# The last pair of expert quads gets an order of its own, and its last weights come in column halves

## The reference, cut to what matters

```
a = jnp.einsum('btd,edf->btef', h, w_gate)        # 1024 -> 256, 32 experts
b = jnp.einsum('btd,edf->btef', h, w_up)
act = jax.nn.silu(a) * b * combine[..., None]
moe = jnp.einsum('btef,efd->btd', act, w_down)    # 256 -> 1024
x = x + moe
y = rmsnorm(x, final_norm_w)
```

## Time and profile before

| what | value |
|---|---|
| median of 3 runs | 655.6 us (653.7 to 657.87) |
| the profiled execution, its own time | 657.37 us |
| its span (first to last instruction) | 655.7 us |
| mean granted TensorE clock | 0.955 of full |
| busy share of the span | PE 88%, DVE 39%, ACT 22%, POOL 11% |
| moved by DMA | 156.44 MB, mean 239 GB/s |

### The profile page before, as it was taken

How to read it: one execution, slowest core, us unless ns; L and a number is a source line. 1 busy time by engine, 2 the same in 40 slices (tenths; PEclk the granted TensorE clock), 3 DMA queues, 4 the chain that set the end, 5 groups by cost and what they waited for, 6 DMA issues and landing times.

```text
span 655.7 us, 11160 instructions
## 1 busy us (share of the span) xinstructions
PE 575.9 (88%) x4490; PEld 401.3 (61%) x4490; DVE 255.6 (39%) x696; ACT 146.1 (22%) x409; POOL 71.6 (11%) x164
## 2 busy tenths in 40 slices
PE   5999999888999999999869999999949677696974
PEld 4777777665777775567757688875434435253531
DVE  4464445651433616234452224544404040404134
ACT  3255333224552001123320013300000000000003
POOL 5000000022411090000100042210000000000000
PEclk8999999999999999999979999999969797988998
DMA  9943333447824062239235892689999999999961
GB/s 265 324 141 95 118 119 120 136 144 190 236 81 153 10 210 73 66 106 278 67 96 178 322 405 108 254 337 421 410 420 422 419 421 420 421 422 419 385 257 73
DMA packets 79435, 156.44 MB, mean 239 GB/s; under 512 B 11042, under 2 KB 64407, under 8 KB 66910
## 3 DMA queue, kind: packets, MB, share of 16 engines
q1 hardware_dynamic: 56880, 142.68, 57.6%
q10 hardware_dynamic: 22505, 13.05, 7.3%
HBM read 147.95 MB, written 7.95 MB: 238 GB/s over the span
## 4 chain that ended last, share of the span: by engine, by line
PE 68%; DMA 22%; DVE 4%; issue 1%; SPq 1%; ACT 1%; ACTq 1%; DVEq 0%
PE ps L1091 30%; DMA arena<-in_w_up_dram 18%; PE ps L1612 7%; PE ps L1471 5%; PE ps L1489 4%; PE ps L1427 2%; PE ps L1053 2%; DMA arena<-in_w_down_dram 2%; PE ps L1668 2%; PE ps L1622 2%; DMA arena<-in_w_in_dram 2%; PE ps L1684 1%; SPq L431 1%; PE ps L1237 1%; PE ps L1201 1%
## 5 line engine op out<-in xcount | busy, mean ns | idle before, releaser
L1091 PE MATMUL ps<-arena 128*128 128x288 f32 x832 | 221.4, 416 | 2.7 <-DMA arena<-in_w_in_dram 2.7
L1091 PEld LDWEIGHTS ps<-arena 128*128 128x128 f32 x832 | 154.0, 192 | 49.3 <-issue 4.9
L1612 PE MATMUL ps<-arena 128*32 128x256 f32 x1024 | 68.6, 430 | 35.8 <-DMA arena<-in_w_up_dram 34.8
L1612 PEld LDWEIGHTS ps<-arena 128*32 128x32 f32 x1024 | 39.6, 124 | 63.6 <-issue 49.7
L1053 PE MATMUL ps<-arena 128*128 128x128 f32 (+6 forms) x172 | 33.2, 300 | 18.5 <-DVE arena L2260 4.7
L1772 DVE SCALAR_TENSOR_TENSOR arena<-arena 128x312 f32<-128x312 f32 x72 | 39.2, 544 | 2.5
L1053 PEld LDWEIGHTS ps<-arena 128*128 128x128 f32 (+6 forms) x172 | 22.0, 156 | 29.2 <-issue 13.1
L1622 PE MATMUL ps<-arena 128*128 128x128 f32 x336 | 38.6, 275 | 0.0
L1622 PEld LDWEIGHTS ps<-arena 128*128 128x128 f32 x336 | 38.1, 192 | 0.0
L1668 PE MATMUL ps<-arena 128*32 128x512 f32 x256 | 30.8, 623 | 3.9 <-DMA arena<-in_w_down_dram 3.9
L1471 PE MATMUL ps<-arena 128*128 128x288 f32 x128 | 31.3, 407 | 0.9 <-DVE arena L2105 0.9
(11 more groups left out here) (368 smaller groups left out, 642.3 us busy)
## 6 DMA issues: line engine op xcount, KB each, us to landing
arena<-in_w_gate_dram SPq DMA_DIRECT2D x32, 1024.0 KB, 18.2
arena<-in_w_up_dram SPq DMA_DIRECT2D x32, 1024.0 KB, 18.5
arena<-in_w_down_dram SPq DMA_DIRECT2D x32, 1024.0 KB, 18.5
arena<-in_w_in_dram SPq DMA_DIRECT2D x26, 1024.0 KB, 5.4
arena<-in_w_branch_delta_dram SPq DMA_DIRECT2D x4, 1024.0 KB, 5.4
out_dram<-arena ACTq DMA_DIRECT2D x8, 512.0 KB, 4.0
arena<-in_w_out_dram SPq DMA_DIRECT2D x4, 1024.0 KB, 5.3
arena<-in_state_delta_dram ACTq DMA_DIRECT2D x7, 512.0 KB, 7.1
```

The lines of the kernel that those rows point to most:

```text
L1091: last = mm(ps[n % 2][:, 0:T], w[:, k, P * (n % 2):P * (n % 2) + P], hT[:, k, :], start=(k == 0), stop=(k == KD - 1))
L1612: last = mm(to[CAP * e:CAP * e + CAP, 0:FE], xgT[u][:, k, CAP * e:CAP * e + CAP], w[e][:, k, :], start=(k == 0), stop=(k == KD - 1))
```

## The change: what it does

For the last pair alone, three things. TensorE's order becomes: gates 6, gather of quad 7, ups 6, flips 6, gates 7, down 6, way back 6, ups 7, flips 7, first half of down 7, pieces 0 and 1, second half of down 7, pieces 2 to 4. ScalarE and VectorE follow in orders that fit. The down weights of quad 7 go into the slots of the even gates, which are free after gates 6, so SyncE waits on `m_gate` rather than on `m_dn1`. And each of those four tables comes in two loads of 512 KiB, first the columns 0 to 511 of all four experts, then the columns 512 to 1023, with a semaphore for each half.

```diff
+LAST_DOWNS = EVEN_GATES
...
-            ups_downs(end * 2 - 1, ((end - 1) % (QUADS // 2)) * (2 * QE) + QE)
+            last = ((end - 1) % (QUADS // 2)) * (2 * QE) + QE
+            ups(end * 2 - 1, last)
+            sp.wait_ge(S["m_gate"], end * 2 - 1)
+            for half in range(2):
+                cols = slice(512 * half, 512 * half + 512)
+                for e, s in enumerate(LAST_DOWNS):
+                    src = w_down[0, bass.ds(last + e, 1)].rearrange("e a b -> (e a) b")
+                    sp.dma_start(slots[s].rearrange("p (a n) -> p a n", a=2)[:, :, cols],
+                                 src.rearrange("(p a) n -> p a n", a=2)[:, :, cols]).then_inc(S[f"last_in{half}"], 16)
...
+            def last_pair(i):
+
+                q = 2 * i
+                gate_silu(q, 0)
+                rows_in(q + 1, 1)
+                flipped(q, 0)
+                gate_silu(q + 1, 1)
+                down_evac(q)
+                flipped(q + 1, 1)
+                down_evac(q + 1)
...
+            def last_pair(i):
+
+                q = 2 * i
+                gate_products(i, 0)
+                gather_next(q)
+                up_products(i, 0)
+                act_flips(q, 0)
+                gate_products(i, 1)
+                pe.wait_ge(S["m_aTev"], q + 1)
+                pe.wait_ge(S["m_dnA"], q)
+                pe.wait_ge(S["m_dnV"], q)
+                loaded(DOWNS, i, 0)
+                for half in range(2):
+                    down_half(0, DOWNS, half)
+                way_back(q, 0, range(NY))
+                up_products(i, 1)
+                act_flips(q + 1, 1)
+                pe.wait_ge(S["m_aTev"], q + 2)
+                pe.wait_ge(S["last_in0"], 16 * QE)
+                down_half(1, LAST_DOWNS, 0)
+                way_back(q + 1, 1, range(2))
+                pe.wait_ge(S["last_in1"], 16 * QE)
+                down_half(1, LAST_DOWNS, 1)
+                way_back(q + 1, 1, range(2, NY))
...
+            def last_pair(i):
+
+                q = 2 * i
+                rows_in(q + 1, 1)
+                gated_rows(q, 0)
+                down_evac(q)
+                add_pieces(q, 0, range(NY))
+                next_place(q * TURN + FIRST_TURNS)
+                way_back(q * TURN + (FIRST_TURNS + 1))
+                gated_rows(q + 1, 1)
+                add_pieces(q + 1, 1, range(2))
+                down_evac(q + 1)
+                add_pieces(q + 1, 1, range(2, NY))
```

More of the change, by code:

```diff
@@ L437, in gates, with ups @@
                     part_load(q, w_gate, first + e, s)
-            def ups_downs(q, first):
+            def ups(q, first):
                 sp.wait_ge(S["m_up"], q)
@@ L442, in ups_downs @@
                     part_load(q, w_up, first + e, s)
+            def ups_downs(q, first):
+                ups(q, first)
                 sp.wait_ge(S["m_dn1"], q)
@@ L1008, in quad_acts, with flipped, down_evac @@
                 nc.scalar.activation(sg[u], ps[2][:, 0:FE], ACT.Silu).then_inc(S["m_sg"], 1)
+            def flipped(q, u):
                 act.wait_ge(S["m_aT"], q + 1)
                 nc.scalar.activation(actT[u].rearrange("p c t -> p (c t)"), ps[4][:, 0:FE], ACT.Copy).then_inc(S["m_aTev"], 1)
-                if not final:
-                    rows_in(q + 1, 1 - u)
+            def down_evac(q):
                 act.wait_ge(S["m_dn0"], q + 1)
@@ L1028, in _ @@
                     quad_acts(i, u)
-            for u in range(2):
-                quad_acts(end - 1, u, final=(u == 1))
+            last_pair(end - 1)
             nc.scalar.activation(t4[:, 0, 0:1], t4[:, 0, 0:1], ACT.Sqrt)
@@ L1634, in spot_rows, with gate_products @@
                     last.then_inc(S["rows_pe"], 1)
-            def quad_products(i, u, final=False):
+            def gate_products(i, u):
                 q = 2 * i + u
@@ L1644, in quad_products, with act_flips @@
                 products(i, u, UPS, ps[3]).then_inc(S["m_up"], 1)
[L1645 to L1648, removed]
+            def act_flips(q, u):
                 pe.wait_ge(S["m_act"], q + 1)
@@ L1654, in quad_products, with down_half, way_back @@
                 last.then_inc(S["m_aT"], 1)
[L1655 to L1674, removed]
+            def down_half(u, table, half):
+                for c in range(2):
+                    for e in range(QE):
+                        w = slots[table[e]].rearrange("p (c n) -> p c n", c=2)
+                        last = mm(ps[5 + half][CAP * e:CAP * e + CAP, :], actT[u][:, c, CAP * e:CAP * e + CAP],
+                                  w[:, c, 512 * half:512 * half + 512], start=(c == 0), stop=(c == 1))
+                last.then_inc(S[f"m_dn{half}"], 1)
+            def way_back(q, u, pieces):
+                for j in pieces:
+                    t, half = PIECES[j]
                     bank = ps[4 if (NY * u + j) % 2 else 7]
+                    if j == 0:
+                        pe.wait_ge(S["m_back"], q + 1)
+                        pe.wait_ge(S["m_dnA"], q + 1)
                     wait_from(S["m_yadd"], q * NY + (j - 1))
@@ L1695, in _ @@
                     quad_products(i, u)
-            for u in range(2):
-                quad_products(end - 1, u, final=(u == 1))
+            last_pair(end - 1)
             pe.wait_ge(S["m_yadd"], end * (2 * NY))
@@ L2252, in next_place, with gated_rows @@
                 dve.wait_ge(S["turns"], turns + 1)
-            def quad_acts(i, u, final=False):
-                q = 2 * i + u
+            def gated_rows(q, u):
                 dve.wait_ge(S["m_sg"], q + 1)
@@ L2261, in quad_acts, with down_evac, add_pieces @@
                                 ps[3][:, 0:FE].rearrange("p (q c) -> p c q", c=2), ALU.mult).then_inc(S["m_act"], 1)
+            def down_evac(q):
+                dve.wait_ge(S["m_dn1"], q + 1)
+                wait_from(S["m_y"], q * NY)
+                V.tensor_copy(dn[:, 512:1024], ps[6][:, :]).then_inc(S["m_dnV"], 1)
+            def add_pieces(q, u, pieces):
+                for j in pieces:
+                    t, half = PIECES[j]
+                    bank = ps[4 if (NY * u + j) % 2 else 7]
+                    dve.wait_ge(S["m_y"], q * NY + (j + 1))
+                    v = x2s if t == 2 else x2[:, t, 512 * half:512 * half + 512]
+                    V.tensor_tensor(v, v, bank[:, 0:v.shape[1]], ALU.add).then_inc(S["m_yadd"], 1)
+            def quad_acts(i, u):
+                q = 2 * i + u
+                gated_rows(q, u)
                 if isinstance(q, int) and q == 0:
@@ L2267, in quad_acts @@
                     way_back(1 + NT)
[L2268 to L2279, removed]
+                rows_in(q + 1, 1 - u)
+                down_evac(q)
+                add_pieces(q, u, range(NY))
                 next_place(q * TURN + FIRST_TURNS)
```

30 lines of the change are left out of this document (28 added, 2 removed).

## The result

| what | before | after |
|---|---|---|
| median of 20 runs each, side by side | 658.91 us | 654.81 us |
| lowest | 653.7 us | 650.89 us |
| the profiled execution, own time | 657.37 us | 653.19 us |
| its span | 655.65 us | 651.47 us |
| mean granted TensorE clock | 0.955 | 0.961 |

The ratio is 0.9941, with a 95% interval of 0.992 to 0.9962: 0.6% faster, or 3.9 us of 658.91. The sign was forecast, and the case "within 1%" was the likelier one; the forecast of 6.3 us was too large, and 654.81 lies outside the range of 647.7 to 652.0. One run of each kernel lies far above the rest (706.17 and 1886.05 us); these two count as slow and are left out of the ratio. One part of that gap is no part of the change: the kernel before has a median of 658.91 over 20 runs, where the three shown ahead of the prediction gave 655.6.

The account below looks back on a forecast made before the run. Transfers were taken to bound the expert part. Stream 2.0 us, down products 3.5 and pieces less copy 0.8 summed to 6.3 us, so 655.6 - 6.3 = 649.3 us, range 647.7 to 652.0.

Parts of the forecast that it names:

- within 1%: Whole kernel: outcome class of a time within 1% (6.56 us) of before; chance 0.58, against 0.38 faster and 0.04 slower.
- 2.9 us of stall: Last four down loads: issued too late at 620.78, taking 12.8 us instead of 9.9; the change removes this 2.9 us.
- rival (a): New waits or load stream: clock drops or slowest DMA engine loses 1.2 us; gain 3.7 to 5.3, near 651; chance 0.22.
- packet price: Half loads of quad 7's down weights: 2 KB runs cost 2.71 us per MiB, against 2.48 for full loads.
- the term of 2.0 us: End of the weight stream: last landing at 634.8 instead of 636.8, a gain of 2.0 us.
- 3.5 + 0.8 = 4.3 us: Behind the last landing: down products shrink by 3.5 us; pieces 0 and 1, less the once-hidden copy, give 0.8.
- TensorE ready in time: Last pair: pieces 0 and 1 end at 634.2, before half 1's weights at 634.8; TensorE idles some 0.6 us.
- SyncE's issue: Issue of the eight half loads: 0.54 us each, 4.4 us in all, from about 610 to 614.5, hidden.
- The clock: TensorE, 600 to 640: full clock despite idle stretches of 1.6 us before down 6 and 1.8 before up 7.
- (b): Half loads: 2 KB packets cost nothing and TensorE is just ready; gain about 7.0 us, 648.6; chance 0.13.
- (c): Split down loads: half 0 lands hardly before half 1 as engines spread; gain near 2.6 us, 653; chance 0.06.
- (d): Half loads far under 387 GB/s: gain used up at 245, 1% slower (662) at 180; chance 0.04 including other losses.

Follow-up runs that it names:

- e3: Changed kernel's order for the last pair, but quad 7's down weights as before: full loads into down slots, undivided down 7; ratio 0.9985 [0.9955, 1.0015].
- e7: Changed kernel, but quad 7's down weights in four full loads into the early gate slots and down 7 undivided; ratio 1.0002 [0.9982, 1.0022].
- e1: The kernel before, unchanged, run again for a second profile; ratio 1.000 [0.9974, 1.0026].
- e8: The kernel before, unchanged, one execution for a third profile; 49.25 us from the landing of quad 6's last up load to the end.
- e11: The kernel before, unchanged, one execution for a fourth profile; 49.65 us from the landing of quad 6's last up load to the end.
- e12: The kernel before, unchanged, one execution for a fifth profile; 49.4 us from the landing of quad 6's last up load to the end.
- e5: The kernel before plus up to 48 gather-shaped matmuls with unread results between gates 6 and ups 6; ratio 1.0021 [1.0002, 1.0041].
- e14: The changed kernel, unchanged, run once more for another profile; ratio 0.9903 [0.9866, 0.994] from six runs.
- e10: Changed kernel with the half loads in the usual down slots, issued only when down 6 is done; ratio 0.9916 [0.9888, 0.9944].
- e9: Changed kernel with half 1 of quad 7's down weights cut again into two 256-column parts, each with own products, copy and pieces; ratio 0.9945 [0.9921, 0.9968].
- e16: Changed kernel with half 1 of quad 7's down weights cut again into two 256-column parts, run a second time; ratio 0.9946 [0.9917, 0.9975].

## Why the prediction was right in its mechanism and wrong in its time

**The absolute time.** "655.6 - 6.3" took a median of three runs as the kernel's. Of 20 it is 658.91, 3.3 us higher, and that alone moves 649.3 to 652.6, out of the range. The prediction counted 0.9 us for such scatter.

**The stream: the step that failed.** It reads: "their issue at 620.78 came too late. That is 2.9 us of stall, and the change removes it". The 2.9 us are in that profile, but they are not the kernel's, and most of them are not the issue's. Against the 29.75 of e3 and e7, the last landing of before is late by 2.9, 1.6, 0.6, 1.0 and 0.7 us: a median of 1.0 and a mean of 1.4. When each of the four last loads lands, in us behind U, tells more (the semaphore updates in the traces have it; the last up load lands 19.8 behind U in each):

| profile | issued from | load 1 | load 2 | load 3 | load 4 |
|---|---|---|---|---|---|
| before | 16.6 | 24.10 | 27.76 | 30.24 | 32.68 |
| e1, before | 16.5 | 23.01 | 25.50 | 28.88 | 31.32 |
| e8, before | 16.0 | 22.92 | 25.38 | 27.87 | 30.33 |
| e11, before | 15.9 | 22.99 | 26.00 | 28.32 | 30.76 |
| e12, before | 15.9 | 23.02 | 25.49 | 27.99 | 30.44 |
| e5, filler ahead of ups 6 | 14.0 | 22.35 | 24.84 | 27.31 | 29.76 |
| e3, new order | 13.8 | 22.32 | 24.80 | 27.27 | 29.73 |

A load costs 2.48 us when nothing is missing, as in e3 and e5. The late issue shows in load 1, which comes 3.1 to 3.2 us behind the ups in four profiles of before: 0.6 to 0.7 us of stall, and no more with an issue from 16.5 (e1) than from 15.9. The rest are jumps in single loads: about 1.1 us in load 1 and 1.2 in load 2 of the first profile, 0.9 in load 3 of e1, 0.5 in load 2 of e11. They belong to a few of the DMA engines: in the first profile 13 of the 16 parts of the last load were in by 30.35 and the last came at 32.68; in e12 all 16 were in by 30.44. So the prediction named such a loss, 1.2 us, in rival (a) for the changed kernel, and overlooked that its own profile of before had such losses in it. Why an engine falls behind stays open, and so does whether a timely issue helps against it: e3, e5 and the changed kernel (30.50 to 30.54 in three profiles) show no jump, but e8 and e12, issued late, show none either.

That a timely issue removes the issue's part is shown by e3 and e5 (e7 lands at 29.77 too). The packet price was sized well: half 0 and half 1 took 5.42 + 5.19 = 10.61 us against 9.92 for four full loads, 0.7 us where 0.9 was reckoned, and the landing is 30.54 behind U against 29.75. So the term of 2.0 us measured 0.3 (median) to 0.6 (mean).

The Trainium skill, page Perfetto Trace Analysis, section DMA Optimizations, ties the benefit of splitting to DMA engines that are generally idle. For the stream the runs agree: at a share of 1.01 the split cost 0.7 us. For the kernel it paid all the same, by what TensorE could do before the second half was in (e7 against the changed kernel: 4.2 us from U to the end).

**Behind the last landing: right.** 3.5 + 0.8 = 4.3 us were forecast. From the landing to the last add it was 10.35 to 10.55 us and is 5.89: 4.5 to 4.7. The forecast had 10.39 and 6.1 for the two. Half 1 took 1.97 rather than 1.81. The tail was forecast to move as a whole, and grew by 0.2 us (8.44 to 8.67). In sum 0.3 to 0.6, plus 4.6, less 0.2: 4.6 to 5.0 us, the gain seen in the profiles. The 3.9 us of the runs, with an interval of 2.5 to 5.3, agree with it.

**TensorE ready in time: right.** Gather in the wait (600.15 to 605.8), ups 6 in 3.66, pieces 0 and 1 done at 636.7, half 1 at 636.96. Counted from U, half 1 was forecast for 30.9 and came at 30.6. The cover was thinner than reckoned: the pieces end 0.2 us ahead of the landing here and together with it in e14, where half 1 still starts only 0.05 us behind its weights.

**SyncE's issue: wrong without cost.** 4.4 us were reckoned for the eight half loads, and they took 13.5, with single issues of 3.47 and 4.45 us. They ended near 626, and half 0 was due at 631.7, half 1 at 636.9, so that it stayed hidden. e10 bears this out: its issue ends at 626.8 and nothing moves.

**The clock: right for this kernel.** It is full from 600 to 640, and the forecast's two waits came at 1.32 and 1.95 us. The weight of 0.22 for rival (a) was fair for its mechanism (e9 shows it), too high for its result. The Trainium skill, page TensorE: Matmul & The Clock Gate, section HAM oscillation, speaks of waits on DMA between short bursts as what lowers the clock; e3, e5 and e7, with 3.5 to 5.1 us of idle ahead of down 7, agree. The same wait of 1.98 us went both ways in e9 and e16, and no run here shows what decides it. Rivals (b), (c) and (d) fell: packets did cost, half 0 landed 5.2 us ahead of half 1, and no load came near 245 GB/s.

## What to carry to other kernels

When a stream of loads sets the end, count what is left to do after the last byte: cutting the last load so that half of that work can go ahead was worth 4.5 us here, although the stream itself became 0.7 us slower, and it needed the engine to be free by then. An earlier landing alone was worth next to nothing (0.3 to 0.5 us by the profiles of e3 and e7, nothing by the times), as the waiting engine lost its clock and paid most of it back. And before a stall in one profile is priced, look at the same stretch in two or three executions, measured from a point that both kernels share, and at the landing of each load in it: a late issue moves the first of them, a slow DMA engine can move any.

## What the runs showed of the hardware that was not expected

**The same code ahead of the change does not take the same time.** U lies between 604.14 and 609.71 us in profiles of one kernel. Part of it is the clock around 340 us. Busy time by stretch (PEclk is the last but two), before and then e12, the same kernel:

```profile
345.00:349.00 4.00, 4.00 (x18) 3.16 (x17) 0.91 (x2) 0.00 (x0) 0.00 (x0) 1.00 0.84 282
```

```profile
345.00:349.00 4.00, 3.17 (x7) 2.32 (x8) 0.78 (x2) 0.00 (x0) 0.95 (x1) 0.50 0.50 141
```

In one execution the clock is back at full there, in the other still at half, and TensorE gets through 7 matmuls rather than 18. Between VectorE's instructions at 343 and at 390 us e12 loses 1.8 us on the first profile. Another 1.5 are lost between 121 and 140 us, where the clock is 0.70 over 133 to 137 in e12 and 1.00 in the first profile. Smaller shifts of either sign make the rest of the 4.2 us. Which course an execution takes was not controlled, and the difference is larger than many an edit's gain.

**Issues that grow.** The branch-pool loads issued in 0.54 us each; the half loads of the changed kernel took up to 4.45 us, issued at 614.73 and 618.39 while the up loads ahead of them landed only by 626.30; the same eight took 5.96 us in all when issued 8 us later (e10), against 13.53 there. The last of the eight ends 19.7 to 19.8 us behind U in either case, just ahead of the landing of the ups at 19.9. A limit on what a queue may hold would fit; no run tried it alone.

**Small packets.** Full loads move 420 to 421 GB/s, the halves, in runs of 2 KB, 391 over 628 to 629, near the branch-pool loads' 387.
